# Gate and up weights of the experts loaded as 256 rows by 1024 columns instead of 512 rows by 512 columns

## The chip, the cores and the metric

The kernel runs on one core of a Trainium2 chip. The metric is the device time of one execution in microseconds (us). The engines are TensorE (PE, its weight loads PEld), VectorE (DVE), ScalarE (ACT), GpSimd (POOL) and SyncE (SP); SP issues nearly all transfers from HBM, which run on the core's 16 DMA engines.

## The reference, cut to what matters

Two layers of a decoder on 256 tokens of width 1024, all in float32. The change touches only the last part, the mixture of experts: eight experts, each with gate and up weights of 1024 x 3584 and down weights of 3584 x 1024.

```python
def swiglu(h, w_gate, w_up, w_down):
    return (jax.nn.silu(h @ w_gate) * (h @ w_up)) @ w_down

def moe_swiglu(h, w_router, b_router, w_gate, w_up, w_down):
    ...
    for e in range(N_EXPERTS):
        y = y + combine[:, e:e + 1].astype(h.dtype) * swiglu(ht, w_gate[e], w_up[e], w_down[e])
```

## The kernel before

Every weight matrix is cut into chunks of 1 MiB, 128 partitions x 2048 float32. A chunk passes through four engines in turn. SP loads it into one of seven slots of `raw` (`RAW = 7`). ACT copies it, rounded to the short format that TensorE multiplies fast, into one of six slots of `w_hi` (`esplit`, L565). DVE subtracts and leaves the rest in `w_lo`, which lies in the same memory as `raw` (L1132). PE multiplies with both parts, and counts the chunk in `mm_done`. SP loads into a slot again when `mm_done` says that PE is through with its old chunk, so at most seven chunks are in transfer or in work; ACT needs `mm_done` of the chunk six back. Every engine walks through its own list of instructions in order; a wait holds up all that stands behind it.

An expert has `EXPERT_CHUNKS = 42` chunks. Chunks 0 to 27 (`DOWN = 28`) are gate and up: seven tiles of 512 columns (`NT`), each of two gate chunks and two up chunks of 512 rows, so that a row of a load has 2048 bytes. Chunks 28 to 41 are down, 256 rows of 1024 columns each, 4096 bytes a row. The experts are ordered by the number of their tokens. The first four (`large`) hold up to 128 tokens and PE does three products of 512 columns for each 128 x 512 piece of weights (L1329 to L1331), 12 a chunk. The last four (`small`) hold up to 64; the two halves of the tokens' values sit side by side in `a_hi`, and two products do (L1733, L1734), 8 a chunk.

In `large`, for tile j: when the gate chunks are done ACT takes Silu of the bank (`sge`, L596); when the up chunks are done DVE multiplies (`he`); PE transposes (`turn_large`, L1666), ACT and DVE split the result into `e_hi` and `e_lo`, which down multiplies with. In `small`, ACT copies the gate bank and the up bank in one go once all four chunks are done (L627, L628), PE folds the halves together (`turn_small`, 16 short products, L1678), ACT takes Silu (`sT`), DVE multiplies (`hT`, L1227), and both split (`e_hi`, L632 and L1232). Where this work stands in an engine's list is written by hand: it follows the split of chunk k of the same expert. For instance, in `small` of ACT:

```python
if k % 4 == 1 and 5 <= k <= DOWN + 1:
    j = (k - 5) // 4
    act.wait_ge(mm_done, C_MOE + 4 * j + 4 + i * EXPERT_CHUNKS)
```

So ACT, having split chunk 4j+5, waits until PE is done with chunk 4j+3, and only then splits chunk 4j+6: the wait stands two chunks behind. In `large` the waits for Silu, for the product and for `e_hi` stand three chunks behind. The PSUM banks of gate and up alternate between 2, 3 and 0, 1 with j; down uses banks 0 and 1, and the picking of the next expert's tokens (`gather`, `turn_block`, `turn_pick`) and the way back (`bring_back`, `add_back`, `result`) use 4 to 7.

Of the kernel before, what the change touches and what calls it, by code (L numbers as in the profile page):

```python
# [60 lines left out]
BRING_AT, PICK_AT, TURN_AT, GATHER_AT = 3, 16, 6, DOWN + 5  # L61
# [6 lines left out]
def hybrid_trunk(nc, x, rel_bias, mix_norm_e, w_in_e, moba_q_norm, moba_k_norm, dsa_q_norm,  # L68
# [34 lines left out]
    with ExitStack() as ctx:  # L103
# [118 lines left out]
        def gate_bank(j):  # L222
            return 2 * ((j + 1) % 2)

        def up_bank(j):
            return gate_bank(j) + 1
# [8 lines left out]
        def _(sp):  # L235
# [16 lines left out]
            def expert_weights(i, e):  # L252
                for k in range(EXPERT_CHUNKS):
                    slot = (C_MOE + k) % RAW

                    sp.wait_ge(mm_done, C_MOE + k - RAW + 1 + i * EXPERT_CHUNKS)
                    if k < 4 * FE_TILES:
                        w = (w_gate_o, w_up_o)[k // 2 % 2]
                        src = w[0][bass.ds(e, 1), (k % 2) * 512:(k % 2) * 512 + 512, (k // 4) * NT:(k // 4 + 1) * NT]
                    else:  # L260
                        q = k - 4 * FE_TILES
                        src = w_down_o[0][bass.ds(e, 1), q * 256:(q + 1) * 256, :]
                    src = src.rearrange("a (k p) n -> p (a k) n", p=P)
                    sp.dma_start(raw[:, slot, :].rearrange("p (k n) -> p k n", k=src.shape[1]), src)\
                        .then_inc(raw_full[slot], 16)
# [27 lines left out]
        def _(act):  # L293
# [293 lines left out]
            def large(i, n, follow, then=P):  # L587

                for k in range(ELEAD, EXPERT_CHUNKS + ELEAD * follow):
                    esplit(i, k)  # L590
                    if k % 4 == 0 and 4 <= k <= DOWN:
                        j = k // 4 - 1
                        act.wait_ge(mm_done, C_MOE + 4 * j + 2 + i * EXPERT_CHUNKS)
                        if j >= 2:
                            act.wait_ge(sem("moe_mul"), j - 1 + n * FE_TILES)
                        nc.scalar.activation(sge[:, j % 2, :], PS[:, gate_bank(j), :], ACT.Silu).then_inc(sem("moe_silu"), 1)  # L596
                    if k % 4 == 1 and 9 <= k <= DOWN + 5:
                        j = (k - 9) // 4
# [12 lines left out]

            def small(i, n, follow):

                for k in range(ELEAD, EXPERT_CHUNKS + ELEAD * follow):
                    esplit(i, k)
                    if k % 4 == 1 and 9 <= k <= DOWN + 5:
                        j = (k - 9) // 4
# [11 lines left out]
                    if k % 4 == 3 and 11 <= k <= DOWN + 7:  # L629
                        j = (k - 11) // 4  # L630
# [50 lines left out]
        def _(dve):  # L681
# [499 lines left out]
            def large(i, n, follow, alone=False, then=P):  # L1181

                for k in range(ELEAD, EXPERT_CHUNKS + ELEAD * follow):
# [3 lines left out]
                    if k % 4 == 2 and 6 <= k <= DOWN + 2:  # L1187
                        j = (k - 6) // 4
                        dve.wait_ge(sem("moe_silu"), j + 1 + n * FE_TILES)
                        dve.wait_ge(mm_done, C_MOE + 4 * j + 4 + i * EXPERT_CHUNKS)  # L1190
# [4 lines left out]
                    if k % 4 == 3 and 11 <= k <= DOWN + 7:  # L1195
                        j = (k - 11) // 4
# [19 lines left out]
            def small(i, n, follow):  # L1216

                for k in range(ELEAD, EXPERT_CHUNKS + ELEAD * follow):
# [3 lines left out]
                    if k % 4 == 2 and 10 <= k <= DOWN + 6:  # L1222
                        j = (k - 10) // 4
                        dve.wait_ge(sem("sm_silu"), j + 1 + n * FE_TILES)
                        if j >= 2:
                            dve.wait_ge(sem("sm_hi"), j - 1 + n * FE_TILES)
                        nc.vector.tensor_tensor(hT[:, j % 2, :], PS[:, 6 + j % 2, 4 * HALF:8 * HALF], sT[:, j % 2, :], ALU.mult)\  # L1227
                            .then_inc(sem("sm_mul"), 1)
                    if k % 4 == 0 and 12 <= k <= DOWN + 8:
                        j = (k - 12) // 4  # L1230
# [96 lines left out]
        def _(pe):  # L1327
# [368 lines left out]
            def large(i, n, follow, alone=False):  # L1696
                pe.wait_ge(sem("moe_xlo"), 2 * i + 2)
                for k in range(EXPERT_CHUNKS):
                    if k < DOWN:
                        j, w, kh = k // 4, k // 2 % 2, k % 2  # L1700
                        if j >= 2 and kh == 0:
                            pe.wait_ge(sem("moe_silu" if w == 0 else "moe_mul"), j - 1 + n * FE_TILES)

                        def body(hi, lo):
                            for kk in range(4):
                                dc = 4 * kh + kk
                                ins = product(PS[:, gate_bank(j) + w, :], a_hi[:, dc, 0:P], a_lo[:, dc, 0:P],
# [3 lines left out]
                    else:  # L1711
                        q = k - DOWN
                        if q % 2 == 0:
                            pe.wait_ge(sem("moe_alo"), q // 2 + 1 + n * FE_TILES)
# [11 lines left out]
                    if k % 4 == TURN_AT % 4 and TURN_AT <= k < TURN_AT + 4 * FE_TILES:  # L1726
                        turn_large(i, n, (k - TURN_AT) // 4, alone)
# [8 lines left out]
            def small(i, n, follow):  # L1736
                pe.wait_ge(sem("moe_xlo"), 2 * i + 2)
                for k in range(EXPERT_CHUNKS):
                    if k < DOWN:
                        j, w, kh = k // 4, k // 2 % 2, k % 2  # L1740
                        if j >= 2 and w == 0 and kh == 0:
                            pe.wait_ge(sem("sm_ev"), j - 1 + n * FE_TILES)

                        def body(hi, lo):
                            for kk in range(4):
                                dc = 4 * kh + kk
                                ins = both(PS[:, gate_bank(j) + w, :], a_hi[:, dc, 0:P], hi[:, kk, :], lo[:, kk, :],
# [3 lines left out]
                    else:  # L1751
                        q = k - DOWN
                        if q % 2 == 0:
# [12 lines left out]
                    if k % 4 == TURN_AT % 4 and TURN_AT <= k < TURN_AT + 4 * FE_TILES:  # L1766
                        turn_small(i, n, (k - TURN_AT) // 4)
# [87 lines left out]
```

## Time and profile before

| | |
|---|---|
| Time, median of 3 (lowest to highest) | 1471.54 us (1471.29 to 1471.98) |
| Profiled execution: its time | 1472.38 us |
| its span, first to last instruction | 1470.7 us |
| busy in the span: PE, PEld, DVE, ACT | 1352.4, 1090.6, 1147.3, 975.1 us |
| mean granted TensorE clock | 0.973 of full |
| moved by DMA | 422.65 MB |

Busy times of different engines overlap. A group of instructions is named by its line, its engine, and output <- input. "Landing" is the time from the issue of a transfer by SP until all of it has arrived.

### The profile page before, as it was taken

Reading aid. Unit: us, or ns where it says so; the run is one execution under the profiler, and the core shown is the slowest. Engines: PE = TensorE matmul, PEld = TensorE weight load, DVE = VectorE, ACT = ScalarE, POOL = GpSimd, SP = SyncE. Lnnn points to the kernel's source line nnn. Section 1 sums busy time; section 2 is a strip of 40 time slices with the busy share of each in tenths; the row PEclk is TensorE's granted clock in tenths of the full one; section 3 lists DMA queues with packets and bytes.
Section 4 is the critical chain, followed back from the end, with each engine's and each line's share of the span. In section 5 each row is a group of like instructions: output and inputs, shape, how many; then the busy total and the mean of one; then the engine's idle time right before and its main releaser. Section 6 shows DMA issues by size and latency. Waiting matters only on the chain.

```text
span 1470.7 us, 17934 instructions
## 1 busy us (share of the span) xinstructions
PE 1352.4 (92%) x6369; PEld 1090.6 (74%) x6370; DVE 1147.3 (78%) x1167; ACT 975.1 (66%) x992; POOL 39.1 (3%) x47
## 2 busy tenths in 40 slices
PE   6987999999779899999999999999889889889886
PEld 5764778888766778888888888888766766676674
DVE  4676354452675489888988979998999999999996
ACT  4445362452577377786777777767788888888884
POOL 1004000000004000000000000000000000000000
PEclk9996999999989889999999999999999999999998
DMA  8550355464340469999999999999999999999995
GB/s 318 193 172 1 125 171 191 126 218 134 123 157 1 143 221 368 368 354 351 369 344 357 367 351 351 369 369 351 387 402 392 387 401 395 387 401 395 387 399 202
DMA packets 184065, 422.65 MB, mean 287 GB/s; under 512 B 7888, under 2 KB 14790, under 8 KB 184006
## 3 DMA queue, kind: packets, MB, share of 16 engines
q1 hardware_dynamic: 182908, 419.10, 78.7%
q0 software_dynamic: 864, 2.68, 0.5%
q8 instruction: 36, 0.59, 0.2%
q14 instruction: 23, 0.19, 0.0%
q10 hardware_dynamic: 234, 0.09, 0.0%
HBM read 420.77 MB, written 1.07 MB: 287 GB/s over the span
## 4 chain that ended last, share of the span: by engine, by line
PE 70%; DVE 12%; ACT 7%; DMA 6%; issue 4%; ACTq 0%; POOL 0%; DVEq 0%; SPq 0%
PE PS L1329 18%; PE PS L1331 18%; PE PS L1330 18%; DVE w_lo L1132 7%; ACT w_hi L565 4%; PE PS L1733 4%; PE PS L1734 3%; DMA raw<-in_w_gate_o_dram 2%; PE PS L1678 2%; DMA raw<-in_w_down_o_dram 2%; DMA raw<-in_w_up_o_dram 2%; DVE w_lo L697 1%; ACT he L628 1%; PE PS L1666 1%; PE PS L1624 1%
## 5 line engine op out<-in xcount | busy, mean ns | idle before, releaser
L1132 DVE TENSOR_TENSOR w_lo<-raw,w_hi 128x2048 fp32r<-128x2048 f32 x336 | 763.1, 2288 | 82.2 <-ACT w_hi L565 79.2
L565 ACT ACTIVATE w_hi<-raw 128x2048 fp32r<-128x2048 f32 x336 | 628.2, 1910 | 35.0 <-DMA raw<-in_w_gate_o_dram 16.8
L1329 PE MATMUL PS<-w_hi,a_hi 128*128 128x512 f32 (+5 forms) x864 | 334.4, 387 | 12.3 <-DVE w_lo L697 6.6
L1331 PE MATMUL PS<-w_hi,a_lo 128*128 128x512 f32 (+5 forms) x864 | 330.7, 383 | 0.0
L1330 PE MATMUL PS<-w_lo,a_hi 128*128 128x512 f32 (+5 forms) x864 | 329.9, 382 | 0.0
L1733 PE MATMUL PS<-w_hi,a_hi 128*128 128x512 f32 x448 | 184.1, 411 | 33.9 <-DVE w_lo L1132 33.4
L1329 PEld LDWEIGHTS PS<-w_hi,a_hi 128*128 128x128 f32 x864 | 164.7, 191 | 44.3 <-issue 10.2
L1331 PEld LDWEIGHTS PS<-w_hi,a_lo 128*128 128x128 f32 x864 | 164.6, 191 | 31.0
L1330 PEld LDWEIGHTS PS<-w_lo,a_hi 128*128 128x128 f32 x864 | 164.7, 191 | 29.3
L1734 PE MATMUL PS<-w_lo,a_hi 128*128 128x512 f32 x448 | 175.7, 392 | 0.0
L697 DVE TENSOR_TENSOR w_lo<-raw,w_hi 128x2048 fp32r<-128x2048 f32 (+4 forms) x70 | 138.9, 2018 | 27.7 <-ACT w_hi L304 27.4
L1733 PEld LDWEIGHTS PS<-w_hi,a_hi 128*128 128x128 f32 x448 | 84.1, 188 | 72.9 <-DVE w_lo L1132 56.6
L304 ACT ACTIVATE w_hi<-raw 128x2048 fp32r<-128x2048 f32 (+4 forms) x70 | 114.9, 1698 | 12.6 <-PE PS L1331 12.6
L1733 PE MATMUL PS<-w_hi,e_hi 128*128 128x512 f32 x224 | 91.9, 410 | 10.4 <-DVE w_lo L1132 9.8
L1734 PEld LDWEIGHTS PS<-w_lo,a_hi 128*128 128x128 f32 x448 | 84.3, 188 | 15.5
L1329 PE MATMUL PS<-w_hi,e_hi 128*128 128x512 f32 x224 | 89.0, 397 | 0.0
L1734 PE MATMUL PS<-w_lo,e_hi 128*128 128x512 f32 x224 | 88.1, 393 | 0.0
L1331 PE MATMUL PS<-w_hi,e_lo 128*128 128x512 f32 x224 | 88.0, 393 | 0.0
L1330 PE MATMUL PS<-w_lo,e_hi 128*128 128x512 f32 x224 | 87.7, 392 | 0.0
L1733 PEld LDWEIGHTS PS<-w_hi,e_hi 128*128 128x128 f32 x224 | 42.1, 188 | 30.6 <-DVE w_lo L1132 18.1
L596 ACT ACTIVATE sge<-PS 128x512 f32<-128x512 f32 x28 | 16.8, 599 | 70.1 <-PE PS L1331 70.1
L316 ACT ACTIVATE a_hi<-PS,gain 128x256 fp32r<-128x256 f32 x32 | 12.6, 478 | 63.1 <-PE PS L1367 60.8
(282 smaller groups left out, 1422.6 us busy)
## 6 DMA issues: line engine op xcount, KB each, us to landing
raw<-in_w_gate_o_dram SPq DMA_DIRECT2D x112, 1024.0 KB, 6.4
raw<-in_w_up_o_dram SPq DMA_DIRECT2D x112, 1024.0 KB, 6.2
raw<-in_w_down_o_dram SPq DMA_DIRECT2D x112, 1024.0 KB, 6.8
raw<-in_w_in_e_dram SPq DMA_DIRECT2D x12, 1024.0 KB, 7.8
raw<-in_w_down_e_dram SPq DMA_DIRECT2D x11, 1024.0 KB, 5.0
raw<-in_w_gate_e_dram SPq DMA_DIRECT2D x10, 1024.0 KB, 5.0
raw<-in_w_up_e_dram SPq DMA_DIRECT2D x10, 1024.0 KB, 5.1
raw<-in_w_out_e_dram SPq DMA_DIRECT2D x4, 1024.0 KB, 5.2
```

Of the source, the lines that this page charges most:

```text
L304: nc.scalar.activation(w_hi[:, c % STG, 0:n], raw[:, c % RAW, 0:n], ACT.Copy).then_inc(hi_done, 1)
L565: nc.scalar.activation(w_hi[:, c % STG, :], raw[:, c % RAW, :], ACT.Copy).then_inc(hi_done, 1)
L596: nc.scalar.activation(sge[:, j % 2, :], PS[:, gate_bank(j), :], ACT.Silu).then_inc(sem("moe_silu"), 1)
L628: nc.scalar.activation(he[:, j % 2, :], PS[:, up_bank(j), :], ACT.Copy).then_inc(sem("sm_ev"), 1)
L697: nc.vector.tensor_tensor(w_lo[:, c % RAW, 0:n], raw[:, c % RAW, 0:n], w_hi[:, c % STG, 0:n], ALU.subtract).then_inc(lo_done, 1)
L1132: nc.vector.tensor_tensor(w_lo[:, c % RAW, :], raw[:, c % RAW, :], w_hi[:, c % STG, :], ALU.subtract).then_inc(lo_done, 1)
L1329: nc.tensor.matmul(dst, xh, wh, start=first, stop=False)
L1330: nc.tensor.matmul(dst, xh, wl, start=False, stop=False)
L1331: return nc.tensor.matmul(dst, xl, wh, start=False, stop=last)
L1678: ins = nc.tensor.matmul(PS[:, 6 + j % 2, at:at + HALF], halves[:, j % 2, f * P:(f + 1) * P], fold[:, :], start=True, stop=True)
L1733: nc.tensor.matmul(dst, xs, wh, start=first, stop=False)
L1734: return nc.tensor.matmul(dst, xs, wl, start=False, stop=last)
```

## The change

Gate and up tiles 0 to 5 are taken in pairs. A pair is eight chunks: four of gate, then four of up, each 256 rows by 1024 columns, 4096 bytes a row, as down has them. Tile 6, the last, is left as it was: two gate and two up chunks of 512 rows and 512 columns. The number of chunks, their bytes and the number of products stay. Within a chunk PE now goes from one bank to the other after each piece of 512 columns, in `body`, as it does in down. Gate pairs are in banks 2 and 3, up pairs in 0 and 1, tile 6 in 4 and 5; so three waits of PE are new or moved: for the emptied gate bank or up bank at chunks 8, 12, 16, 20, for `moe_back` at chunk 24, and for tile 5's up bank at chunk 28.

`units(k, done, late)` gives the tiles whose work stands behind chunk k: those with `done(u) + late + u % 2 == k`. Both tiles of a pair are done at one time; the work of the odd one stands one chunk later.

```diff
-        def gate_bank(j):
-            return 2 * ((j + 1) % 2)
+        def gate_bank(u):
+            return 2 + u % 2 if u < FE_TILES - 1 else 4
+        def up_bank(u):
+            return u % 2 if u < FE_TILES - 1 else 5
+        def gates_at(u):
+            return 8 * (u // 2) + 4 if u < FE_TILES - 1 else DOWN - 2
+        def ups_at(u):
+            return 8 * (u // 2) + 8 if u < FE_TILES - 1 else DOWN
+        def units(k, done, late):
+            return [u for u in range(FE_TILES) if done(u) + late + u % 2 == k]
...
SP
-                    if k < 4 * FE_TILES:
+                    if k < DOWN - 4:
+                        w = (w_gate_o, w_up_o)[k // 4 % 2]
+                        src = w[0][bass.ds(e, 1), (k % 4) * 256:(k % 4) * 256 + 256, (k // 8) * D:(k // 8 + 1) * D]
+                    elif k < DOWN:
                         w = (w_gate_o, w_up_o)[k // 2 % 2]
-                        src = w[0][bass.ds(e, 1), (k % 2) * 512:(k % 2) * 512 + 512, (k // 4) * NT:(k // 4 + 1) * NT]
+                        src = w[0][bass.ds(e, 1), (k % 2) * 512:(k % 2) * 512 + 512, FFE - NT:FFE]
...
ACT, large
-                    if k % 4 == 0 and 4 <= k <= DOWN:
+                    for j in units(k, gates_at, 2):
...
-                    if k % 4 == 1 and 9 <= k <= DOWN + 5:
+                    for j in units(k, ups_at, 5):
...
ACT, small
-                    if k % 4 == 1 and 5 <= k <= DOWN + 1:
-                        j = (k - 5) // 4
-                        act.wait_ge(mm_done, C_MOE + 4 * j + 4 + i * EXPERT_CHUNKS)
+                    for j in units(k, gates_at, 2):
+                        act.wait_ge(mm_done, C_MOE + gates_at(j) + i * EXPERT_CHUNKS)
                         if j >= 2:
                             act.wait_ge(sem("sm_tr"), j - 1 + n * FE_TILES)
-                        nc.scalar.activation(sge[:, j % 2, :], PS[:, gate_bank(j), :], ACT.Copy)
+                        nc.scalar.activation(sge[:, j % 2, :], PS[:, gate_bank(j), :], ACT.Copy).then_inc(sem("sm_eg"), 1)
+                    for j in units(k, ups_at, 1):
+                        act.wait_ge(mm_done, C_MOE + ups_at(j) + i * EXPERT_CHUNKS)
                         nc.scalar.activation(he[:, j % 2, :], PS[:, up_bank(j), :], ACT.Copy).then_inc(sem("sm_ev"), 1)
...
PE, small (large alike, with product in place of both)
+                    if k < DOWN - 4:
+                        j, w, kq = k // 8, k // 4 % 2, k % 4
+                        if j >= 1 and kq == 0:
+                            pe.wait_ge(sem("sm_eg" if w == 0 else "sm_ev"), 2 * j + n * FE_TILES)
+                        def body(hi, lo):
+                            for kk in range(2):
+                                dc = 2 * kq + kk
+                                for half in range(2):
+                                    cols = slice(half * NT, (half + 1) * NT)
+                                    ins = both(PS[:, 2 * (1 - w) + half, :], a_hi[:, dc, 0:P], hi[:, kk, cols], lo[:, kk, cols],
+                                               dc == 0, dc == DC - 1)
+                            return ins
+                        echunk(i, k, 2, D, body)
...
-                    if k % 4 == TURN_AT % 4 and TURN_AT <= k < TURN_AT + 4 * FE_TILES:
-                        turn_small(i, n, (k - TURN_AT) // 4)
+                    for j in units(k, ups_at, 2):
+                        turn_small(i, n, j)
```

The last loads of the first expert on SP (L264, `raw` <- the weights in HBM, with the shape for 128 partitions), in order: before, gate and up alternate in twos, seven times each, and then comes down.

```order
L264 DMA raw<-in_w_gate_o_dram 128x4x512 x2
L264 DMA raw<-in_w_up_o_dram 128x4x512 x2
L264 DMA raw<-in_w_gate_o_dram 128x4x512 x2
L264 DMA raw<-in_w_up_o_dram 128x4x512 x2
L264 DMA raw<-in_w_down_o_dram 128x2x1024 x14
```

With the change they alternate in fours, three times each, with a shape of 2 x 1024 for each partition, and a last tile in twos as before.

```order
L277 DMA raw<-in_w_gate_o_dram 128x2x1024 x4
L277 DMA raw<-in_w_up_o_dram 128x2x1024 x4
L277 DMA raw<-in_w_gate_o_dram 128x4x512 x2
L277 DMA raw<-in_w_up_o_dram 128x4x512 x2
L277 DMA raw<-in_w_down_o_dram 128x2x1024 x14
```

What moved: up chunks of a tile come four places behind its gate chunks, not two, and two tiles are complete at once.

ACT's list at the start of the last expert, in `small` (`w_hi` is the split of a chunk, the first row's two are chunks 4 and 5). Before:

```order
L565 ACTIVATE w_hi<-raw 128x2048 x2
L627 ACTIVATE sge<-PS 128x512
L628 ACTIVATE he<-PS 128x512
L565 ACTIVATE w_hi<-raw 128x2048 x4
L621 ACTIVATE sT<-PS 128x256
L627 ACTIVATE sge<-PS 128x512
L628 ACTIVATE he<-PS 128x512
L565 ACTIVATE w_hi<-raw 128x2048 x2
L632 ACTIVATE e_hi<-hT 128x4x64
```

With the change (the first row's three are chunks 4 to 6):

```order
L578 ACTIVATE w_hi<-raw 128x2048 x3
L636 ACTIVATE sge<-PS 128x512
L578 ACTIVATE w_hi<-raw 128x2048
L636 ACTIVATE sge<-PS 128x512
L578 ACTIVATE w_hi<-raw 128x2048 x2
L639 ACTIVATE he<-PS 128x512
L578 ACTIVATE w_hi<-raw 128x2048
L639 ACTIVATE he<-PS 128x512
L578 ACTIVATE w_hi<-raw 128x2048 x3
L631 ACTIVATE sT<-PS 128x256
L578 ACTIVATE w_hi<-raw 128x2048
L631 ACTIVATE sT<-PS 128x256
```

What moved: the two copies `sge` and `he` that stood together behind every fourth split, two chunks behind PE, are now apart. The `sge` of a pair stand behind splits 6 and 7 and need chunk 3; the `he` stand behind splits 9 and 10 and need chunk 7. The `he` of an even tile thus still stands two chunks behind the one it needs, once in eight chunks; the other three copies stand three or four behind.

## Rows read from the trace of the kernel before

**Rows 1.** The page: busy times, and GB/s in 40 slices of the span.

```profile
PE 1352.4 (92%) x6369; PEld 1090.6 (74%) x6370; DVE 1147.3 (78%) x1167; ACT 975.1 (66%) x992; POOL 39.1 (3%) x47
...
GB/s 318 193 172 1 125 171 191 126 218 134 123 157 1 143 221 368 368 354 351 369 344 357 367 351 351 369 369 351 387 402 392 387 401 395 387 401 395 387 399 202
```

**Rows 2.** Stretches, all engines: start:end length, busy us of each, PEclk, DMA share, GB/s.

```profile
core 0: us, PE busy (x) PEld busy (x) DVE busy (x) ACT busy (x) POOL busy (x), PEclk, DMA share, GB/s
700.00:800.00 100.00, 100.00 (x453) 82.38 (x452) 87.83 (x58) 73.52 (x52) 0.00 (x0) 1.00 0.98 355
1183.00:1294.78 111.78, 100.09 (x474) 77.85 (x474) 104.63 (x70) 92.66 (x76) 0.00 (x0) 1.00 1.04 394
```

**Rows 3.** Waits by engine, 600 to 1000 us: us in total, times, longest.

```profile
ACT sge L596 <- PE PS L1331: 50.2, 19, 4.7
DVE w_lo L1132 <- ACT w_hi L565: 49.0, 46, 2.8
```

**Rows 4.** Timeline of SP in the large experts: start, us, ... x count.

```profile
710.66 39.42 SPq L264 DMA_DIRECT2D raw<-in_w_down_o_dram  x14
...
833.73 39.42 SPq L264 DMA_DIRECT2D raw<-in_w_down_o_dram  x14
```

**Rows 5.** DMA issues, 640 to 680 us: count, KB each, median us to landing.

```profile
raw<-in_w_gate_o_dram SPq DMA_DIRECT2D x8, 1024.0 KB, 5.1
```

**Rows 6.** Timeline of SP in the small experts.

```profile
1015.94 2.20 SPq L264 DMA_DIRECT2D raw<-in_w_up_o_dram  x2
...
1183.01 36.69 SPq L264 DMA_DIRECT2D raw<-in_w_down_o_dram  x14
...
1294.78 36.66 SPq L264 DMA_DIRECT2D raw<-in_w_down_o_dram  x14
...
1406.43 35.26 SPq L264 DMA_DIRECT2D raw<-in_w_down_o_dram  x14
```

**Rows 7.** DMA from 1140 to 1180 us: gate and up.

```profile
DMA packets 7794, 15.48 MB, mean 387 GB/s; under 512 B 237, under 2 KB 237, under 8 KB 7794
```

**Rows 8.** DMA from 1190 to 1220 us: down.

```profile
DMA packets 3211, 12.27 MB, mean 409 GB/s; under 512 B 189, under 2 KB 189, under 8 KB 3211
```

**Rows 9.** Timeline of ACT in a small expert, behind its first gate chunks.

```profile
1230.57 1.92 ACT L565 ACTIVATE w_hi<-raw 128x2048 fp32r<-128x2048 f32 x1 [0.79 <-DMA raw<-in_w_gate_o_dram]
...
1238.70 1.92 ACT L565 ACTIVATE w_hi<-raw 128x2048 fp32r<-128x2048 f32 x1 [0.79 <-DMA raw<-in_w_up_o_dram]
```

**Rows 10.** Chain that ended last, 1056 to 1068 us: start, us, what.

```profile
1056.56 0.45 issue
1057.01 0.59 ACT he L628
1057.60 1.81 ACT w_hi L565
...
1059.44 2.30 DVE w_lo L1132
...
1061.79 0.50 PE PS L1733
...
1063.90 1.73 PE PS L1678 x16
...
1067.61 0.45 issue
```

**Rows 11.** Timeline of DVE in the small experts.

```profile
1220.89 8.90 DVE L1132 TENSOR_TENSOR w_lo<-raw,w_hi 128x2048 fp32r<-128x2048 f32 x4
```

**Rows 12.** Timeline of PE, large expert, gate and up: two products 27 apart.

```profile
649.73 0.39 PE L1331 MATMUL PS<-w_hi,a_lo 128*128 128x512 f32 x1
...
655.85 0.39 PE L1331 MATMUL PS<-w_hi,a_lo 128*128 128x512 f32 x1
```

**Rows 13.** Timeline of PE, large expert, down: two products 13 apart.

```profile
728.02 0.39 PE L1330 MATMUL PS<-w_lo,e_hi 128*128 128x512 f32 x1
...
731.00 0.39 PE L1331 MATMUL PS<-w_hi,e_lo 128*128 128x512 f32 x1
```

More of the change, by code:

```diff
@@ L615, in small @@
                     esplit(i, k)
-                    if k % 4 == 1 and 9 <= k <= DOWN + 5:
-                        j = (k - 9) // 4
+                    for j in units(k, ups_at, 5):
                         act.wait_ge(sem("sm_tr"), j + 1 + n * FE_TILES)
@@ L1194, in large @@
                             .then_inc(sem("moe_mul"), 1)
-                    if k % 4 == 3 and 11 <= k <= DOWN + 7:
-                        j = (k - 11) // 4
+                    for j in units(k, ups_at, 7):
                         dve.wait_ge(sem("moe_ahi"), j + 1 + n * FE_TILES)
@@ L1698, in large @@
                 for k in range(EXPERT_CHUNKS):
[L1699 to L1702, printed above, removed]
+                    if k < DOWN - 4:
+                        j, w, kq = k // 8, k // 4 % 2, k % 4
+                        if j >= 1 and kq == 0:
+                            pe.wait_ge(sem("moe_silu" if w == 0 else "moe_mul"), 2 * j + n * FE_TILES)
+                        def body(hi, lo):
[3 more added lines that the diff above has]
+                                    cols = slice(half * NT, (half + 1) * NT)
+                                    ins = product(PS[:, 2 * (1 - w) + half, :], a_hi[:, dc, 0:P], a_lo[:, dc, 0:P],
+                                                  hi[:, kk, cols], lo[:, kk, cols], dc == 0, dc == DC - 1)
+                            return ins
+                        echunk(i, k, 2, D, body)
+                    elif k < DOWN:
+                        w, kh = k // 2 % 2, k % 2
+                        if k == DOWN - 4:
+                            pe.wait_ge(sem("moe_back"), i + 1)
                         def body(hi, lo):
@@ L1706, in body @@
                                 dc = 4 * kh + kk
-                                ins = product(PS[:, gate_bank(j) + w, :], a_hi[:, dc, 0:P], a_lo[:, dc, 0:P],
+                                ins = product(PS[:, 4 + w, :], a_hi[:, dc, 0:P], a_lo[:, dc, 0:P],
                                               hi[:, kk, :], lo[:, kk, :], dc == 0, dc == DC - 1)
@@ L1725, in large @@
                     between(i, k, follow, alone)
-                    if k % 4 == TURN_AT % 4 and TURN_AT <= k < TURN_AT + 4 * FE_TILES:
-                        turn_large(i, n, (k - TURN_AT) // 4, alone)
+                    for j in units(k, ups_at, 2):
+                        turn_large(i, n, j, alone)
                 if alone:
@@ L1738, in small, with body @@
                 for k in range(EXPERT_CHUNKS):
[L1739 to L1742, printed above, removed]
+                    if k < DOWN - 4:
+                        j, w, kq = k // 8, k // 4 % 2, k % 4
+                        if j >= 1 and kq == 0:
+                            pe.wait_ge(sem("sm_eg" if w == 0 else "sm_ev"), 2 * j + n * FE_TILES)
+                        def body(hi, lo):
+                            for kk in range(2):
+                                dc = 2 * kq + kk
+                                for half in range(2):
+                                    cols = slice(half * NT, (half + 1) * NT)
+                                    ins = both(PS[:, 2 * (1 - w) + half, :], a_hi[:, dc, 0:P], hi[:, kk, cols], lo[:, kk, cols],
+                                               dc == 0, dc == DC - 1)
+                            return ins
+                        echunk(i, k, 2, D, body)
+                    elif k < DOWN:
+                        w, kh = k // 2 % 2, k % 2
+                        if k == DOWN - 4:
+                            pe.wait_ge(sem("moe_back"), i + 1)
                         def body(hi, lo):
@@ L1746, in body @@
                                 dc = 4 * kh + kk
-                                ins = both(PS[:, gate_bank(j) + w, :], a_hi[:, dc, 0:P], hi[:, kk, :], lo[:, kk, :],
+                                ins = both(PS[:, 4 + w, :], a_hi[:, dc, 0:P], hi[:, kk, :], lo[:, kk, :],
                                            dc == 0, dc == DC - 1)
@@ L1765, in small @@
                     between(i, k, follow)
-                    if k % 4 == TURN_AT % 4 and TURN_AT <= k < TURN_AT + 4 * FE_TILES:
-                        turn_small(i, n, (k - TURN_AT) // 4)
+                    for j in units(k, ups_at, 2):
+                        turn_small(i, n, j)
             gather(0)
```

27 lines of the change are left out of this document (11 added, 16 removed).

## The prediction

> **What bounds the kernel now.** I read the stretches first, since a mean over the span mixes stages with different limits, and it is the weights' path that changes. The page shows PE busy for 92% of the span and GB/s that rise in the last third from some 360 to 400 [rows 1]: those are the large and then the small experts. In a stretch of the large ones PE is busy without a gap, at a granted clock of 1.00 (its upper level, 2.4 GHz), and DMA moves 355 GB/s [rows 2]. In the waits of that stage, ACT waits for PE and DVE for ACT; no wait of PE stands there [rows 3]. A large expert takes the time from its first down load to the next one's, 833.73 - 710.66 = 123.1 us [rows 4], and a transfer lands 5.1 us after its issue [rows 5], though SP could have up to seven slots in use: it waits for PE to free them. PE bounds the large experts. What transfers do there costs nothing, as PE's work covers it.
>
> In the small experts, with two products in place of three, PE is busy for 100.1 us of 111.8, DVE for 104.6, and the DMA share is 1.04 at 394 GB/s [rows 2]. An expert takes 1294.78 - 1183.01 = 111.8 and 1406.43 - 1294.78 = 111.65 us [rows 6]. Two things ask for attention here. The rate is 387 GB/s in a stretch of gate and up [rows 7] and 409 in one of down [rows 8]. A chunk of 1.0486 MB thus takes 2.710 us at the one and 2.564 at the other, and 28 x 2.710 + 14 x 2.564 = 111.8 us: exactly the expert's time. And four chunks after another, ACT's splits of gate and up start (1238.70 - 1230.57) / 3 = 2.71 us apart, each after 0.79 us of waiting for the transfer [rows 9]. So the 16 DMA engines bound the small experts: they are never without a queue, and take 5.7% longer for a megabyte in rows of 2048 bytes than in rows of 4096.
>
> There is a second limit close beneath it. Within gate and up, the chain goes round once in four chunks: end of a tile on PE, the copies of both banks, the split of the next chunk, its `w_lo`, two chunks and a fold on PE. From 1056.56 to 1067.61 that is 11.05 us, with 0.45 of issue, 0.59 of `he`, 1.81 of `w_hi`, 2.30 of `w_lo`, and 1.73 of folds [rows 10], where four chunks of transfer take 10.84. The slots even this out: what is late here is caught up in down, where DVE takes four chunks at (8.90 - 2.29) / 3 = 2.20 us each [rows 11].
>
> **The change part by part.** *Row length.* 24 of the 42 chunks of an expert go from 2048 to 4096 bytes a row. The trace shows no load of such rows out of a wider matrix (the rows lie 14336 bytes apart; down's follow one another), so I bound it: nothing, or the whole way to down's rate, 2.710 - 2.564 = 0.146 us a chunk. I take the whole, since row length is the visible difference and the gate loads of today have the same spacing. Where it counts: from about 1016 us on, at chunk 8 of the first small expert [rows 6]. That leaves 16 of its chunks and 3 x 24 of the others, 88. 88 x 0.146 = 12.9 us less. In the large experts the same loads are covered by PE.
>
> *Bytes, products, chunks.* All as before. SP issues as many transfers; nothing for these.
>
> *The chain in gate and up (small).* It now closes once in eight chunks through the `he` copy of the even tile. By rows 10: from the end of a pair's last chunk 0.45 + 0.59 + 1.81 + 2.30 = 5.15 us to the next needed `w_lo`; then on PE that chunk 2.11, a fold 1.73, a chunk 1.98, the other fold 1.73, and four chunks at 8 x 0.23 = 1.84: 20.1 us, against 8 x 2.564 = 20.5 of transfers at the new rate (before: 22.1 against 21.7). It fits, barely. Were the order as before, 22.1 us for eight chunks would stand against 20.5, and much of the gain would be eaten.
>
> *DVE in the small experts.* Its work stays 104.6 us [rows 2]. The new transfers take 38 x 2.564 + 4 x 2.710 = 108.3 us per expert. So it may idle 3.7 us where it could idle 7.2. The two `sT` and the next `sge` now stand close together behind splits 13 and 14, of which the second `sT` waits for the second fold, 5.15 + 2.11 + 1.73 + 1.98 + 1.73 = 12.7 us after the pair's end. With at most 0.59 each for `sT` and `sge` and 1.81 for the split, `w_hi` of chunk 15 comes at 15.7. DVE is through with chunk 14 at 5.15 + 4 x 2.20 = 14.0, and 0.4 later with the `hT` behind it (its work beside the splits is 104.6 - 42 x 2.20 = 12 us in 70 - 42 = 28 instructions). So it stands idle some 1.3 us per pair, 3.9 per expert, against the 3.7 that the transfers leave. Bounds: nothing, if the slots even it out; or 1 us more for other such places, 1.2 beyond the transfers. I take 0.5 us per small expert, 2 us.
>
> *PE in the large experts.* Its new waits: for `sge` and `he` of a pair before the next pair. These stand at or before split 11 on ACT and DVE, and PE cannot start chunk 12 before DVE has split it, behind them in the same list; nothing. `moe_back` is set behind DVE's split 20, chunk 24 asks for it; nothing. Waits of ACT and DVE for PE stay three chunks behind for even tiles and are four for odd ones. From the end of the awaited chunk, the next split is through on ACT and DVE after 0.45 + 0.6 + 1.9 + 2.3 = 5.3 us, and PE comes to it after three chunks of 12 x 0.227 = 2.7, 8.2 us: cover 2.9 us. In each chunk PE changes the bank after every third product. Down does that today: 13 products later is 2.98 us, 0.2292 each [rows 13], against 6.12 / 27 = 0.2267 in gate and up [rows 12]. Were all of it the bank, 288 products x 0.0025 x 4 experts = 2.9 us more; at the other end nothing. I take 0.5.
>
> Sum: -12.9 + 2 + 0.5 = -10.4. Against the profiled execution's 1472.4 us (span 1470.7 and 1.7 around it) that gives 1462.0; the median of the runs is 0.8 lower, so 1461.
>
> A rule of the Trainium skill gives a smaller gain. In "DMA: Bandwidth & Descriptors", section "Why small descriptors are slow (HBM only)", each packet costs some 3 cycles beside its 32-byte beats. By that, an estimate, 2 x 67 cycles become 131, 2.2% in place of 5.7, and the first term would be 5.3 us. The trace's 387 and 409 do not agree with it, unless something else than row length parts them.
>
> **The rivals.**
> 1. *The work behind the transfers takes over.* DVE loses the 3.9 us per expert and 1.3 more behind the `he` copy and at the start, where four adds fall between its splits: 104.6 + 5.2 = 109.8 per expert, 2.0 less than now. Over the 3.7 experts (88 of 24 chunks each) that is 7.4 less, and 0.5 goes to PE: 1465. For it: 104.6 of 108.3 [rows 2]. Against it: the slots lend some chunks.
> 2. *Only a part of the 5.7% is row length*, the rest being that down's rows follow one another in memory. Half: 6.4 - 1 for the small costs, 1466. The rule just cited would come out about there.
> 3. *The new loads run at 387 as before*: the row length isn't what matters. Then nothing is left but a shorter chain that is covered: 1471.5. The skill's same page, section "Where 436 GB/s comes from", has some 358 GB/s of HBM binding such loads, and would have row length change nothing; both rates of the trace lie above that.
> 4. *Slower: the wider rows out of a wide matrix are slower than two short ones.* Half of them start at an odd multiple of 2048 bytes, which no load of today with 4096-byte rows does. At 0.146 us more per chunk in place of less, 88 x 0.146 = 12.9 more, 1484. It decides where such a chunk takes over 2.710 us; each 0.033 us above that is 2.9 us in all. Against it: today's 2048-byte rows start there too, and get 387.
>
> **How the numbers follow.** The main case 0.57, own range 1458 to 1464; rival 1 0.16, rival 2 0.13, rival 3 0.05, rival 4 0.09. The range reaches over rivals 1 and 2 and down to the full 12.9 with a little more for a chain that no longer holds up anything: 1457 to 1468. 0.2%, about what a measurement of this kernel can tell from no change, is 2.9 us. Faster 0.86 (main, 1, 2), same 0.05, slower 0.09.
>
> **What would show it.** Right: gate and up stretches of the small experts near 409 GB/s; 108 to 109 us from one expert's first down load to the next one's, still 123.1 for the large ones; ACT waiting for transfers of gate and up at an expert's start. Rival 1: DMA share below its 1.04 in the small experts, landing times shorter, DVE without idle time beyond its waits for `w_hi`. Rivals 2 to 4: the GB/s of those stretches. The forecast falls if the large experts take longer than 123.1 us, or if PE waits appear there.

## The result and the profile after

The change makes the kernel faster: 1459.2 us, median of 4 (1456.44 to 1460.68), against 1471.76. The ratio of the runs to those of before is 0.9903, with a 95% interval of 0.9888 to 0.9919; the two medians divided give 0.9915, which lies inside it. The forecast was 1461 with a range of 1457 to 1468. The profiled execution took 1456.4 us, with a span of 1454.8.

The page after the change, its busy times, its GB/s and its count of packets, answers to [rows 1]:

```profile
PE 1348.9 (93%) x6369; PEld 1088.9 (75%) x6370; DVE 1144.6 (79%) x1167; ACT 977.3 (67%) x992; POOL 39.2 (3%) x47
...
GB/s 311 206 173 1 118 172 197 122 231 132 110 177 1 136 200 368 367 352 356 366 343 364 362 349 356 371 365 347 406 402 410 409 403 410 410 403 409 409 402 197
DMA packets 134913, 422.65 MB, mean 291 GB/s; under 512 B 7888, under 2 KB 14790, under 8 KB 134854
```

The bytes are the same and the packets fewer, 134913 for 184065. GB/s in the last third are now above 400 nearly throughout. A stretch of the large experts, and one small expert from its first down load to the next one's, in the columns of [rows 2]:

```profile
700.00:800.00 100.00, 100.00 (x453) 82.40 (x453) 87.96 (x56) 73.73 (x52) 0.00 (x0) 1.00 0.97 357
1175.63:1283.73 108.10, 100.43 (x475) 77.94 (x475) 103.80 (x70) 92.42 (x76) 0.00 (x0) 1.00 1.03 407
```

The large experts are as they were, PE without a gap. In the small one PE and DVE do the same work in 3.7 us less, and the DMA share stays above 1, 1.03 for 1.04, at 407 GB/s for 394. SP's first down load of each expert, large and then small, as in [rows 4, 6]:

```profile
585.15 39.16 SPq L277 DMA_DIRECT2D raw<-in_w_down_o_dram  x14
...
708.02 39.36 SPq L277 DMA_DIRECT2D raw<-in_w_down_o_dram  x14
...
953.87 39.36 SPq L277 DMA_DIRECT2D raw<-in_w_down_o_dram  x14
...
1066.77 35.45 SPq L277 DMA_DIRECT2D raw<-in_w_down_o_dram  x14
...
1175.63 35.09 SPq L277 DMA_DIRECT2D raw<-in_w_down_o_dram  x14
...
1283.73 35.05 SPq L277 DMA_DIRECT2D raw<-in_w_down_o_dram  x14
...
1391.86 33.14 SPq L277 DMA_DIRECT2D raw<-in_w_down_o_dram  x14
```

A large expert takes 122.9 us (708.02 - 585.15; 123.1 before), the third and the fourth small one 108.10 and 108.13 (111.77 and 111.65 before). ACT's list behind the first gate loads of a small expert shows the transfers' pace, as [rows 9] did:

```profile
1221.27 1.92 ACT L578 ACTIVATE w_hi<-raw 128x2048 fp32r<-128x2048 f32 x1 [0.64 <-DMA raw<-in_w_gate_o_dram]
...
1228.95 1.92 ACT L578 ACTIVATE w_hi<-raw 128x2048 fp32r<-128x2048 f32 x1 [0.65 <-DMA raw<-in_w_gate_o_dram]
```

The splits start (1228.95 - 1221.27) / 3 = 2.56 us apart where it was 2.71, and each waits 0.63 to 0.65 us for its transfer. So the transfers still set the pace. The waits of ACT and DVE from 1060 to 1440 us:

```profile
ACT w_hi L578 <- DMA raw<-in_w_up_o_dram: 16.0, 36, 0.7
DVE w_lo L1142 <- ACT w_hi L578: 15.2, 27, 2.0
ACT w_hi L578 <- DMA raw<-in_w_gate_o_dram: 11.3, 25, 0.7
ACT e_hi L642 <- DVE hT L1234: 9.2, 12, 1.5
...
ACT sge L636 <- PE PS L1684: 7.0, 4, 2.1
ACT sT L631 <- PE PS L1684: 4.0, 6, 0.8
```

What ACT waits for most is the transfers. The two last lines are waits for folds, which the list of the kernel before, for the same stretch, does not have; more of them below.

Where did the time come from? From the last large expert's first down load to the end of the span, before takes 1470.7 - 956.80 = 513.9 us, after 1454.8 - 953.87 = 500.9: 13.0 less. Two more profiles of the changed kernel have 502.2 and 501.8 there, so the gain is 11.7 to 13.0, against the one profile of before. The three large experts ahead of it give 0.5. The remaining 2.4 of the 15.9 between the two spans lie ahead of the first gate load (422.53 and 420.09), in code that the change does not touch. The two other profiles have that load at 422.34 and 422.92, so this was the luck of one execution, and it is most of what parts the 15.9 from the 12.6 between the medians.

The gain is not spread evenly. From one expert's first down load to the next one's, and from the last one's to the end of the span:

| us | last large to 1st small | 1st to 2nd small | 2nd to 3rd | 3rd to 4th | 4th to the end |
|---|---|---|---|---|---|
| before | 115.24 | 110.97 | 111.77 | 111.65 | 64.3 |
| the change | 112.90 | 108.86 | 108.10 | 108.13 | 62.9 |
| the change, again and third time | 112.65, 112.84 | 109.94, 109.02 | 108.06, 108.10 | 108.11, 108.20 | 63.5, 63.6 |

Only the third and the fourth small expert gain all of the 24 x 0.146 = 3.5 us that the new rows can save in one; the second gains 1.0 to 2.1.

### The profile page after: what moved, and what is told of

It reads as the page before. It is cut to its first block, busy times and chain, and to the rows that moved or that the text cites. A ratio compares the mean times of both kernels' runs of the same rounds, so it can differ in the third digit from the quotient of the medians.

```text
span 1454.8 us, 17923 instructions
## 1 busy us (share of the span) xinstructions
PE 1348.9 (93%) x6369; PEld 1088.9 (75%) x6370; DVE 1144.6 (79%) x1167; ACT 977.3 (67%) x992; POOL 39.2 (3%) x47
## 2 busy tenths in 40 slices
DMA packets 134913, 422.65 MB, mean 291 GB/s; under 512 B 7888, under 2 KB 14790, under 8 KB 134854
## 4 chain that ended last, share of the span: by engine, by line
PE 67%; DVE 15%; ACT 6%; issue 6%; DMA 5%; ACTq 0%; POOL 0%; DVEq 0%; SPq 0%
PE PS L1335 18%; PE PS L1337 18%; PE PS L1336 18%; DVE w_lo L1142 8%; ACT w_hi L578 3%; PE PS L1755 2%; DMA raw<-in_w_gate_o_dram 2%; PE PS L1684 2%; PE PS L1756 2%; DMA raw<-in_w_up_o_dram 2%; DVE w_lo L707 1%; PE PS L1672 1%; PE PS L1630 1%; DMA raw<-in_w_down_o_dram 1%; PE PS L1435 1%
## 5 line engine op out<-in xcount | busy, mean ns | idle before, releaser
L317 ACT ACTIVATE w_hi<-raw 128x2048 fp32r<-128x2048 f32 (+4 forms) x70 | 114.9, 1698 | 12.6 <-PE PS L1337 12.6
L329 ACT ACTIVATE a_hi<-PS,gain 128x256 fp32r<-128x256 f32 x32 | 12.6, 478 | 64.6 <-PE PS L1373 62.4
L484 ACT ACTIVATE sg<-PS,nst 128x512 f32<-128x512 f32 (+1 forms) x12 | 7.2, 650 | 64.5 <-PE PS L1337 64.5
```

The costliest lines, as they stand in the source:

```text
L317: nc.scalar.activation(w_hi[:, c % STG, 0:n], raw[:, c % RAW, 0:n], ACT.Copy).then_inc(hi_done, 1)
```

## The experiments

In the table, "expert" is the time between the first down loads of the second and third, and of the third and fourth small experts, in each one's profile. Ratios are to the kernel before, run beside each group on the same chip; its medians there were 1472.6 to 1473.7 us, so compare ratios rather than medians across groups.

| | time, median | ratio (95% interval) | expert |
|---|---|---|---|
| before | 1471.8 | | 111.77, 111.65 |
| the change | 1459.2 | 0.9903 (0.9888 to 0.9919) | 108.10, 108.13 |
| the change again | 1458.4 | 0.9903 (0.9886 to 0.9920) | 108.06, 108.11 |
| the change, third time | 1459.6 | 0.9902 (0.9885 to 0.9918) | 108.10, 108.20 |
| new order, gate and up rows of 2048 | 1471.8 | 0.9992 (0.9983 to 1.0001) | 111.73, 111.63 |
| down too in rows of 2048 | 1468.0 | 0.9973 (0.9958 to 0.9987) | 110.25, 110.20 |
| long rows in large experts only | 1475.0 | 1.0010 (1.0000 to 1.0020) | 111.78, 111.59 |
| old order, rows of 4096 | 1470.0 | 0.9977 (0.9964 to 0.9990) | 109.86, 109.90 |
| half of `w_lo` left out | 1458.7 | 0.9901 (0.9884 to 0.9918) | 108.15, 108.02 |
| one bank at a time | 1459.4 | 0.9905 (0.9890 to 0.9921) | 108.13, 108.10 |
| down in rows of 1024 | 1483.7 | 1.0074 (1.0057 to 1.0091) | 114.48, 114.41 |
| down in rows of 8192 | 1459.4 | 0.9901 (0.9885 to 0.9918) | 108.20, 108.22 |
| the same, half of `w_lo` left out | 1456.0 | 0.9875 (0.9854 to 0.9897) | 107.05, 106.98 |
| rows of 8192, looser waits | 1455.3 | 0.9868 (0.9833 to 0.9903) | 107.16, 107.24 |

Three theories were on the table. Theory 1: row length sets the rate of transfers, which bound the small experts. Theory 2: the looser chain of copies and waits is the gain. Theory 3: down's higher rate came from its rows following one another in memory.

**The yardstick.** The changed kernel, unedited.

> The changed kernel itself, once more, as the yardstick for the others. If row length and nothing else gave the gain, its small experts take 108.1 us each from down load to down load as in the first profile, and the ratio to before stays near 0.990 or 0.991 (1457 to 1461 us).

1458.4 us, as expected. A third time, beside the second group of runs:

> The changed kernel again beside these three, as their yardstick: 1457 to 1461 us.

1459.6 us. Differences of 1 us between medians mean nothing here; the time of the third or fourth small expert in the profile repeats within 0.1 us, that of the second only within 1.1 (108.86 to 109.94).

**The new order with the old rows.** The banks, waits and places of the change stay; PE's loops over a chunk are changed to match its shape.

```diff
-    src = w[0][e, (k % 4) * 256:(k % 4) * 256 + 256, (k // 8) * D:(k // 8 + 1) * D]
+    src = w[0][e, (k % 2) * 512:(k % 2) * 512 + 512, t * NT:(t + 1) * NT]   # t = 2 * (k // 8) + k // 2 % 2
```

> The order, banks and waits of the change, but gate and up loaded again as 512 rows by 512 columns, 2048 bytes a row, first the one tile of a pair, then the other. Theory 1 (row length is the gain, the transfers bound the small experts): back to 387 GB/s in gate and up, 111.7 us for a small expert, 1471 to 1472 us in all. Theory 2 (the looser chain of copies and waits is the gain): the time stays at 1459 or so. A mixture would lie between, and the share can be read off.

Measured: 1471.8 us, no difference from before, and 111.7 us an expert. The DMA view of its gate and up stretch shows the old rate again:

```profile
DMA packets 6814, 13.54 MB, mean 387 GB/s; under 512 B 204, under 2 KB 204, under 8 KB 6814
```

The order alone gives nothing, which is the end of theory 2 in its simple form.

**Down in short rows too.** Here too PE's loops over a chunk of down match its shape.

```diff
-    src = w_down_o[0][e, q * 256:(q + 1) * 256, :]
+    src = w_down_o[0][e, (q // 2) * 512:(q // 2 + 1) * 512, (q % 2) * NT:(q % 2 + 1) * NT]
```

> The change, and down loaded with 2048 bytes a row (512 rows by 512 columns, one half of the columns after the other). Theory 1: all of an expert now runs at 387 GB/s in down and 409 in gate and up; 14 chunks by 0.146 us make a small expert 2.0 us longer than the change's 108.1, so 110.1, and the whole some 8 us longer, 1466 to 1467. Theory 3 (what parts 409 from 387 is that down's rows follow one another in memory, and the gain came from something else): the down stretch stays near 409 or falls no further than gate and up do. Theory 2 expects no change.

Measured: 110.2 us an expert, as theory 1 had it, and 1468.0 in all, 1 us above what was expected. Its DMA view, gate and up and then down:

```profile
DMA packets 3714, 14.31 MB, mean 409 GB/s; under 512 B 220, under 2 KB 220, under 8 KB 3714
```

```profile
DMA packets 4867, 9.67 MB, mean 387 GB/s; under 512 B 145, under 2 KB 145, under 8 KB 4867
```

The two rates have changed places: 409 with 4096 bytes a row out of the wide matrix, 387 with 2048 out of down's. Theory 3 falls, and the gain per chunk is confirmed from the other side: (110.2 - 108.1) / 14 = 0.15 us.

**Long rows in the large experts only.** The small ones load as in the run with the new order and the old rows.

```diff
-            with sp.Fori(1, NE) as p:
-                expert_weights(p, ...)
+            with sp.Fori(1, PAIRS) as p:
+                expert_weights(p, ...)
+            with sp.Fori(PAIRS, NE) as p:
+                expert_weights(p, ..., True)    # gate and up in rows of 2048 bytes
```

> The rows of 4096 bytes only in the four large experts; the four small ones load gate and up in rows of 2048 bytes as before. Theory 1 (transfers are covered by PE in the large experts): no gain is left, 1471 to 1472 us, large experts at 122.9 to 123.1 us, small at 111.7. If long rows help the large experts, the time lies below that.

Measured: no gain, 1475.0 us, where 1471 to 1472 was expected and the kernel before beside it took 1473.5, with large experts at 122.9 and small ones at 111.7. Where PE covers the transfers, their rate buys nothing. The interval of the ratio begins at 1.0000, so the kernel may be a little slower; the profile shows 1.5 us more behind the last down load than before (65.8 for 64.3), for which I have no cause.

**The old order with the new rows.** The kernel before, its gate and up chunks loaded as 256 rows by 1024 columns: same bytes, same work, but not the weights that the products should have.

```diff
-    src = w[0][e, (k % 2) * 512:(k % 2) * 512 + 512, (k // 4) * NT:(k // 4 + 1) * NT]
+    c0 = min(k // 4 * NT, FFE - D)
+    src = w[0][e, (k % 2) * 256:(k % 2) * 256 + 256, c0:c0 + D]
```

> The kernel before, its order, banks and waits, with every gate and up chunk loaded as 256 rows by 1024 columns of 4096 bytes: the wrong part of the weights for its products, the same bytes and work. Transfers alone would need 42 x 2.564 = 107.7 us for a small expert. Theory A (the old chain of 11.05 us per four chunks in gate and up holds it up, so the new order was needed for the gain): well above that, 109.5 to 110.5 us, 1464 to 1467 in all. Theory B (the slots even it out over the expert, and row length alone gives the gain): 107.7 to 108.2 us, 1456 to 1460.

Measured: 109.9 us an expert, as theory A had it, and 1470.0 in all, above its 1464 to 1467. Only 0.2% of the gain of 1% is left. The view of the chain that ended last:

```profile
1157.40 0.38 issue
1157.78 0.59 ACT he L629
1158.37 1.81 ACT w_hi L566
...
1160.21 2.30 DVE w_lo L1133
...
1162.56 0.50 PE PS L1734
...
1164.66 1.73 PE PS L1679 x16
```

It is the chain of [rows 10], link by link: the copy `he` starts at 1157.78 here, and the ones before and after it start at 1146.58 and 1168.83, 11.1 us for four chunks, where their transfer takes 10.3. From 1140 to 1180 us the transfers still run at 410 GB/s, into the slots that an expert's start leaves free; then down:

```profile
DMA packets 3985, 15.36 MB, mean 384 GB/s; under 512 B 236, under 2 KB 236, under 8 KB 3985
...
raw<-in_w_down_o_dram SPq DMA_DIRECT2D x13, 1024.0 KB, 7.4
```

384 GB/s instead of 409, and 7.4 us to landing where the change's down loads take 9.1: the queue grows shorter, as SP waits for slots. The first small expert takes 1073.83 - 958.57 = 115.3 us as before (115.2), where the change takes 112.9; the third and fourth keep half of the change's gain, 1.9 and 1.75 of 3.67 and 3.52 us. So the whole gain needs both: row length to make the transfers faster, and the new order so that the chain can follow. Over the whole kernel the order alone gives nothing that can be told from zero, and row length alone a quarter. The new order is banks, shapes of chunks and waits at once; no run has the old order with its waits set back, so that it is the waits rests on the chain above and not on a run of their own.

**Less work for DVE.** In the small experts DVE makes `w_lo` for half of each chunk, and PE takes that half twice.

```diff
-                nc.vector.tensor_tensor(w_lo[:, c % RAW, :], raw[:, c % RAW, :], w_hi[:, c % STG, :],
+                nc.vector.tensor_tensor(w_lo[:, c % RAW, 0:n], raw[:, c % RAW, 0:n], w_hi[:, c % STG, 0:n],   # n = CW // 2
```

> In the small experts DVE makes w_lo for only the first half of each chunk (chunks 4 to 41 of each), and PE multiplies the second half with the first half's w_lo: that part of the computation is left out. DVE has some 40 us less to do per expert, PE the same as before. Theory 1 (transfers alone bound the small experts now): nothing changes but the tail behind the last transfer, 108.1 us an expert, 1457 to 1461 us. Rival 1 of the prediction (DVE and its waits already share the bound): an expert gets shorter than 108.1, by a microsecond or more.

Measured: 108.1 us for the third and the fourth small expert and 1458.7 in all, no difference. One expert of it, in the columns of [rows 2]:

```profile
1176.00:1284.00 108.00, 99.41 (x475) 77.97 (x474) 66.03 (x70) 93.10 (x76) 0.00 (x0) 1.00 1.03 407
```

DVE is busy for 66 us of 108 and these experts get no faster. The transfers alone bound the changed kernel there.

It is otherwise where the small experts begin. From the last large expert's first down load to the first small one's this run takes 1067.01 - 955.94 = 111.1 us, where four profiles with all of DVE's work (the change three times, and the next run) have 112.4 to 112.9; from the first small one to the second it takes 108.3, where they have 108.9 to 109.9. From 1010 to 1070 us, the change and then this run, in the columns of [rows 2]:

```profile
1010.00:1070.00 60.00, 57.31 (x278) 46.47 (x277) 57.55 (x37) 50.80 (x42) 0.00 (x0) 1.00 1.02 399
1010.00:1070.00 60.00, 58.56 (x286) 48.00 (x285) 38.12 (x37) 51.83 (x42) 0.00 (x0) 1.00 1.02 400
```

DVE has next to no room there, 57.55 of 60 us, and relieving it takes 1.3 to 1.8 us off that first stretch. In all it is 1.4 to 2.8 us from the last large expert's first down load to the end of the span, too little for the medians to show. So rival 1 of the prediction did not come about in the experts that run on, and did in a small part in the first one or two.

**One bank at a time.** The two loops of a gate or up chunk on PE changed about.

```diff
-                            for kk in range(2):
-                                dc = 2 * kq + kk
-                                for half in range(2):
+                            for half in range(2):
+                                for kk in range(2):
+                                    dc = 2 * kq + kk
```

> The change, with PE doing both products' pieces of one bank before it goes to the other within a gate or up chunk, so it changes bank once a chunk and not three times. The prediction gave the changes of bank 0 to 0.7 us per large expert. The first profile of the change has large experts at 122.9 us with them, 0.15 less than before, so I expect no difference here: 122.9, and 1457 to 1461 in all.

Measured: 1459.4 us and 122.9 a large expert (956.22 - 833.35). Changing banks after every third product costs nothing that can be seen.

**Rows of 1024 bytes.** Down's chunks from 1024 rows of 256 columns, at other places of the matrix than they should be.

```diff
-    src = w_down_o[0][e, q * 256:(q + 1) * 256, :]
+    src = w_down_o[0][e, q // 4 * 640:q // 4 * 640 + 1024, q % 4 * 256:q % 4 * 256 + 256]
```

> The change, with down's chunks loaded as 1024 rows of 256 columns, 1024 bytes a row, from other places of the matrix, so the down products use other weights than they should; sizes and all work as before. A fixed time per row would make a chunk of 1024-byte rows 2.710 + 2 x 0.146 = 3.00 us, an expert 108.1 + 14 x 0.436 = 114.2, the whole some 23 us more than the change. If each halving costs the same 5.7%, 2.865 a chunk, 112.3 an expert, some 16 us more.

Measured: 114.4 us an expert and 1483.7 in all, as a fixed time per row has it. The down stretch:

```profile
DMA packets 8635, 8.71 MB, mean 348 GB/s; under 512 B 133, under 2 KB 8635, under 8 KB 8635
```

**Rows of 8192 bytes.** A partition takes two neighbouring rows of down, and the transposes and folds of `he` and `sge` take every second column to match.

```diff
-                        src = src.rearrange("a (k p) n -> p (a k) n", p=P)
+                        src = src.rearrange("a (p k) n -> p (a k) n", p=P)    # down only
...
-    he[:, j % 2, f * P:(f + 1) * P]
+    he[:, j % 2, f // 2 * 2 * P + f % 2:(f // 2 + 1) * 2 * P:2]
```

> Down loaded with 8192 bytes a row: each partition takes two rows of the matrix that follow one another, and the transposes and folds take every second column to match. If the cost is a fixed time per row of a load, 2 x 2048 to 4096 saved 0.146 us a chunk, and 4096 to 8192 saves half of that, 0.073 us: 14 chunks, 1.0 us an expert, 107.1, 3.7 us in all. If loads are cut into pieces of 4096 bytes anyway, nothing changes and the count of packets stays. PE and ACT as before.

Measured: 108.2 us an expert, no gain, and yet the pieces are not cut at 4096 bytes:

```profile
DMA packets 1130, 8.22 MB, mean 411 GB/s; under 512 B 127, under 2 KB 127, under 8 KB 127
...
raw<-in_w_down_o_dram SPq DMA_DIRECT2D x7, 1024.0 KB, 7.4
```

1130 packets carry what took 2124 in the change, at 411 GB/s. But a load lands after 7.4 us, where the change has 9.1: the queue is short, so something behind the transfers holds them up. I relieved DVE as above to see what the transfers could do:

> Down in rows of 8192 bytes, and DVE relieved as in the run before with half of w_lo left out in the small experts (PE uses the first half's for the second). If DVE hid a gain of the longer rows, an expert now falls below 108.1 us, to 107.1 if the cost is a fixed time per row. If 4096 bytes is where the rate ends, it stays at 108 and the down stretch at 410 GB/s with a full queue.

```profile
DMA packets 1161, 8.45 MB, mean 423 GB/s; under 512 B 129, under 2 KB 129, under 8 KB 129
...
raw<-in_w_down_o_dram SPq DMA_DIRECT2D x7, 1024.0 KB, 10.2
```

107.0 us an expert and 423 GB/s: the gain was there, hidden under the second limit at 108.2.

**The second limit.** In ACT's list of the change stand two kinds of waits for folds, one in gate and up and one at the start of down:

```profile
1151.65 0.39 ACT L631 ACTIVATE sT<-PS 128x256 f32<-128x256 f32 x1 [0.75 <-PE PS L1684]
...
1189.43 0.60 ACT L636 ACTIVATE sge<-PS 128x512 f32<-128x512 f32 x1 [2.09 <-PE PS L1684]
```

The first is that of `sT` behind split 14, of which the prediction spoke; the next pair's, behind split 22, is alike. The other, 2.09 us, it did not see: tile 6's `sge` goes into the buffer of tile 4's, behind split 28, and tile 4's fold stands behind chunk 26. The last kernel moves both one chunk back, with the `hT` and `e_hi` that follow `sT`, on top of the rows of 8192 bytes.

```diff
 ACT, small
-                    for j in units(k, ups_at, 5):
+                    for j in units(k, ups_at, 6):
...
-                    for j in units(k, gates_at, 2):
+                    for j in units(k, lambda u: gates_at(u) + u // 6, 2):
...
-                    for j in units(k, ups_at, 7):
+                    for j in units(k, ups_at, 8):
 DVE, small
-                    for j in units(k, ups_at, 6):
+                    for j in units(k, ups_at, 7):
...
-                    for j in units(k, ups_at, 8):
+                    for j in units(k, ups_at, 9):
```

> Down in rows of 8192 bytes, and in the small experts the waits of ACT on the folds made looser: sT, hT and both halves of e_hi stand one chunk later, and tile 6's sge stands behind split 29 in place of 28, where it waited for tile 4's fold. All work is there. Theory: in the run with 8192-byte rows alone the chain of ACT and DVE, at 108.2 us an expert, hid a transfer time of 107.0. If these waits are that chain, an expert falls to 107.0 to 107.4 us, and the whole 2.5 to 4 us below the change, 1455 to 1457. If DVE's own work (104) and its other waits are, it stays at 108.

Measured: 107.2 us an expert and 1455.3 in all, ratio 0.9868 (0.9833 to 0.9903): full work, and clearly faster than before. Against the change itself the intervals overlap; what speaks for a gain is the expert's 107.2 for 108.1 us, and the time from the last large expert's first down load to the end of the span, 1453.6 - 955.42 = 498.2 us where three profiles of the change have 500.9, 501.8 and 502.2. The waits for folds are gone from its list of waits, so these were what held the rows of 8192 bytes up; DVE was busy for as long as ever, 103.2 us.

## Why the prediction was right

**What bounds.** Right. The large experts are PE's and gained no more than 0.15 us each; the small ones gained the rest, and from the third on they are the transfers' alone.

**Row length, -12.9 us.** Right in mechanism, and in size for the expert that runs on: the whole step from 387 to 409 GB/s came, and 108.3 us were worked out for an expert, 108.1 measured. In the sum luck helped. The term was put together as 2.3 us in the first small expert and 3.5 in each of the others, with nothing behind the last first down load. The profile has 2.3, then 2.1, 3.7 and 3.5, and 1.3 behind: 13.0, which agrees with 12.9 as parts that are off make up for each other. The two other profiles have 11.7 and 12.1 in all.

**The chain.** The prediction had 20.1 us for eight chunks. In the chain of the changed kernel that ended last, the second folds of two pairs stand 20.3 us apart, where the transfers need 20.5:

```profile
1149.89 1.75 PE PS L1684 x16
...
1151.94 0.59 ACT sge L636
1152.53 1.81 ACT w_hi L578
...
1170.15 1.75 PE PS L1684 x16
```

The length is as forecast, the link is not. The prediction closed the round through the `he` copy of the even tile, but ACT's list has no wait of `he` for PE from 1060 to 1440 us. What closes it is the wait of the second `sT` for the odd tile's fold, behind split 14, which the prediction had priced as idle time of DVE; the `sge` and the split above stand right behind it. That 20.3 comes out so near 20.1 is luck.

The prediction also said that in the old order the chain would eat up much of the gain: in the old order 0.23% is left of 0.97%.

**DVE and its waits, +2 us.** It was set in the wrong place. The prediction took 0.5 us for each of four small experts. In the third and the fourth it is nothing: half of the splitting can go and the expert stays at 108.1. In the first and second, DVE's work does cost something, 1.3 to 1.8 and 0.6 to 1.6 us by the run with half of `w_lo`. How much of that the kernel before paid as well, no run shows, so whether the 2 us were too much in all stays open. The idle time in the third is about as worked out, 4.5 us for 3.9, below, and DVE is busy for 103.8 us, 0.8 less than taken; this proves nothing by itself, since busy and idle time add up to the expert's time whatever bounds it.

```profile
  ACT w_hi L578: 4.5, 7
```

**PE in the large experts, +0.5 us.** Mis-sized: 0.15 us less an expert, and none of it from the banks. The 1.8 us by which 1461 lies above 1459.2 are less than the changed kernel's own spread, 1456.44 to 1460.68, and no run divides them among the terms.

**The rivals.** Rival 1, with its 109.8 us an expert and 1465 in all, is refuted by the 108.1 and the run with half of `w_lo`, but it was near: it shows in the first small expert, and with rows of 8192 bytes the engines' waits take over at 108.2. Rivals 2, 3 and 4 fall with the stretch of gate and up at 409 GB/s and more.

The rule from the Trainium skill that was weighed ("DMA: Bandwidth & Descriptors", section "Why small descriptors are slow (HBM only)"), some 3 cycles a packet, would have made the gain 2.2% of a transfer, an estimate. The trace does not agree: 2.71 us became 2.56, which on the same base is 5.4% (the 5.7% of the prediction are of the shorter transfer). The rate of some 358 GB/s in the same page, section "Where 436 GB/s comes from", did not bind either, on this one core.

## What to carry to other kernels

Where the trace shows the DMA engines without a gap, compare the GB/s of stretches with different row lengths before anything else: the difference, times the chunks that are on the bound, was 12.9 us here, against a gain of 11.7 to 13.0. Then work out how long the chain behind the transfers takes for the same chunks. If it has no more room, longer rows give only a part of this until the waits in it are set further back, and the two have to be changed together. Look at the first expert after a stage with another bound by itself, since its limit can be another one than that of the experts that follow. Where another engine covers the transfers, leave them as they are.

## What the runs showed of the hardware

By these runs a load pays a fixed time per row, or per packet, as here each row was one packet. With a full queue, on this one core, 1 MiB over 128 partitions ran at 348 GB/s in rows of 1024 bytes, 387 in 2048, 409 in 4096 and 423 in 8192, that is 3.01, 2.71, 2.56 and 2.48 us a chunk: the steps are 0.30, 0.15 and 0.08. More finely, from the times of an expert over its 14 chunks of down, they are (114.4 - 110.2) / 14 = 0.30, (110.2 - 108.1) / 14 = 0.15 and (108.1 - 107.0) / 14 = 0.08. Over 16 engines this is 0.15 us x 16 / 256 rows = 9.4 ns a row and engine between 2048 and 4096, as much between 1024 and 2048, and some 10 between 4096 and 8192. Whether the rows follow one another or lie 14336 bytes apart made no difference at 4096 bytes, and a packet can be 8192 bytes long. Drawn on to rows without end, an estimate from these numbers, a chunk would take 2.71 - 0.30 = 2.41 us, 435 GB/s. In the Trainium skill, "DMA: Bandwidth & Descriptors", section "Where 436 GB/s comes from", 435.2 GB/s is the limit of the 16 ports; the estimate agrees with that number, though the fastest stretch here had 423.
